# A long chain of layers in one kernel on one core: other start, other order around the recurrent mixer's last turns, other order of the last attention and of its gating, gate sums spread by transpositions

## The reference

```python
def mlstm_layer(h, ...):      # recurrent mixer
    proj = rms_norm(h, norm_g) @ w_in            # q,k | v | o | z | gates
    qk = silu(causal_depthwise_conv(qk, conv_w))
    ht = mlstm_chunkwise(q, k, v, i_pre, log_sigmoid(f_pre))
    ht = rms_norm(sigmoid(o) * ht, hnorm_g)
    return (ht * silu(z)) @ w_out
def dilated_layer(h, k, v, ...):   # last attention: 4 heads, 3 groups of dilation 1, 4, 16
    q, z = split(rms_norm(h, norm_g) @ w_in)
    q = apply_rope(rms_norm(q, qnorm_g), cos, sin)
    o = sum over groups of softmax-weighted dilated_window_attention(q[:, :, g], k, v, ...)
    return (o * silu(z)) @ w_out
def ple_add(h, p_l, ...):
    gate = sigmoid(rms_norm(h, norm_g) @ w_gate)
    return h + (p_l @ w_proj) * gate
```

## Time and profile before

| | us |
|---|---|
| median of 3 runs (1410.26 to 1410.67) | 1410.33 |
| profiled execution | 1411.51 |
| its span, first to last instruction | 1409.7 |
| TensorE busy | 1386.3 |
| VectorE busy | 832.8 |
| ACT busy | 603.5 |
| GpSimd busy | 192.2 |

### The profile page before, as it was taken

One profiled execution on the slowest core, in us unless ns is written; L12 is line 12 of the kernel. 1 busy time (PEld: TensorE's weight loads), 2 busy tenths in 40 slices (PEclk: granted clock), 3 DMA queues, 4 the chain that ended last, 5 costly groups with the idle time before them and its releaser, 6 DMA issues.

```text
span 1409.7 us, 17303 instructions
## 1 busy us (share of the span) xinstructions
PE 1386.3 (98%) x6796; PEld 1125.7 (80%) x6796; DVE 832.8 (59%) x1201; ACT 603.5 (43%) x921; POOL 192.2 (14%) x156
## 2 busy tenths in 40 slices
PE   7999999999999999999999999999999999999998
PEld 5777777878888888888888888877788888787786
DVE  5556656755342797624767355645464666777674
ACT  5254433433235564423444255434454545345461
POOL 3300010212212300000000121000001211244230
PEclk9999999999999999999999999999999999999999
DMA  6221322122353433332333323422124232221141
GB/s 234 75 78 58 90 76 75 61 75 82 104 171 92 134 91 110 106 98 89 93 102 97 118 81 125 123 78 68 61 79 160 90 117 96 75 67 54 45 144 65
DMA packets 37266, 135.39 MB, mean 96 GB/s; under 512 B 4400, under 2 KB 5056, under 8 KB 36672
## 3 DMA queue, kind: packets, MB, share of 16 engines
q1 hardware_dynamic: 37184, 134.28, 30.6%
HBM read 127.97 MB, written 6.29 MB: 95 GB/s over the span
## 4 chain that ended last, share of the span: by engine, by line
PE 93%; DVE 3%; ACT 2%; DMA 1%; POOL 1%; issue 1%; SPq 0%; DVEq 0%; ACTq 0%; POOLq 0%
PE ps L203 91%; PE ps L207 2%; ACT WH L187 1%; DMA raw<-in_wall 1%; DMA cv<-in_cvec 1%; DVE TT L162 1%; SPq L210 0%; POOL PB L150 0%; DVE WL L150 0%; ACT SS L200 0%; DVE SS L174 0%; POOL SQS L150 0%; ACT L200 0%; DVE QT L162 0%; ACT SQ L200 0%
## 5 line engine op out<-in xcount | busy, mean ns | idle before, releaser
L203 PE MATMUL ps<-HH,WH 128*128 128x512 f32 x1088 | 439.9, 404 | 9.4 <-DVE WL L150 8.6
L203 PE MATMUL ps<-HH,WL 128*128 128x512 f32 x1088 | 425.7, 391 | 0.0
L203 PE MATMUL ps<-HL,WH 128*128 128x512 f32 x1088 | 425.1, 391 | 0.0
L150 DVE TENSOR_TENSOR WL<-raw,WH 128x1024 fp32r<-128x1024 f32 x222 | 285.5, 1291 | 78.0 <-ACT WH L187 76.9
L187 ACT CAST WH<-raw 128x1024 fp32r<-128x1024 f32 x222 | 231.5, 1044 | 148.1 <-PE ps L203 128.8
L203 PEld LDWEIGHTS ps<-HH,WH 128*128 128x128 f32 x1088 | 205.2, 189 | 59.5 <-DVE WL L150 8.6
L203 PEld LDWEIGHTS ps<-HH,WL 128*128 128x128 f32 x1088 | 204.9, 188 | 44.3
L203 PEld LDWEIGHTS ps<-HL,WH 128*128 128x128 f32 x1088 | 205.3, 189 | 41.7 <-issue 1.7
L150 POOL TENSOR_TENSOR SQS<-SQS,SQ 128x512 f32<-128x512 f32 x54 | 83.2, 1541 | 701.4 <-ACT SQ L200 687.2
L203 PE MATMUL ps<-PH,WH 128*128 128x512 f32 x424 | 168.1, 396 | 0.8 <-DVE PL L150 0.8
L203 PE MATMUL ps<-PH,WL 128*128 128x512 f32 x424 | 165.2, 390 | 0.0
(11 more groups left out here) (219 smaller groups left out, 1451.5 us busy)
## 6 DMA issues: line engine op xcount, KB each, us to landing
raw<-in_wall SPq DMA_DIRECT2D x222, 512.0 KB, 3.6
kept<-PW SPq DMA_DIRECT2D x2, 2048.0 KB, 9.1
PWR<-kept SPq DMA_DIRECT2D x2, 2048.0 KB, 8.5
X<-in_xT SPq DMA_DIRECT2D x8, 256.0 KB, 5.6
X<-in_xT SPq DMA_DIRECT2D x4, 512.0 KB, 5.3
out_T<-X SPq DMA_DIRECT2D x8, 256.0 KB, 2.0
pe<-in_pT SPq DMA_DIRECT2D x2, 512.0 KB, 4.5
DM<-in_dm SPq DMA_DIRECT2D x1, 640.0 KB, 4.2
```

Of the source, the lines that this page charges most:

```text
L150: return self.put(None if self.e is None else self.e.tensor_tensor(out, x, y, op))
L203: return self.put(None if self.e is None else self.e.matmul(out, l, r, start=start, stop=stop, skip_group_check=True))
```

## The change

The first weight unit is loaded, cast and subtracted in two halves of 512 columns, X tile 1 comes behind it, units 1 and 2 follow X tiles 1 and 3. The sums of squares of the first norm are added by VectorE, not GpSimd. While the first four output tiles run, ACT and VectorE prepare fewer units ahead (`lead = 1`). TensorE runs eleven 32-bit products of 128 x 128 on the mask `rst` before its first real product; their result isn't used. The pooling side work starts one tile later.
In the recurrent mixer `gt` is turned into columns (four small transpositions more, a copy `mcol` on ACT) and spread by four transpositions for each head. The last 16 turns come after the fourth block of the residual.
In the last attention VectorE works on a query product first and ACT squares behind it and frees the bank; the rate is 4.5 instead of 3.9; the row of reciprocals of heads 0 to 2 has another bank; head h is finished after the gate tile h + 1, head 3 within the residual, and the second operation of the gate (`v_silu2_out`) is split off and made one tile later.
The last output tile is computed in two halves of 256 tokens, each with its own chain and its own store.

```diff
@@ -338,6 +339,16 @@
+    def load_half(self, i):
+        sl = slice(512 * i, 512 * i + 512)
+        d = self.dma_start(self.raw[:, 0, sl], self.wall[0, :, sl])
+        if i == 0:
+            d.then_inc("half", sig=self.S.half, by=16)
+        else:
+            d.then_inc(("unit", 0), sig=self.S.raw[0], by=16)
+            self.u = 1
...
@@ -349,6 +360,15 @@
+    def high_half(self, i):
+        sl = slice(512 * i, 512 * i + 512)
+        if i == 0:
+            self.wait_ge(self.S.half, "half")
+        else:
+            self.wait_ge(self.S.raw[0], "unit", 0)
+            self.u = 1
+        self.copy(self.WH[:, 0, sl], self.raw[:, 0, sl]).then_inc(*((["half"], [("unit", 0)])[i]), sig=self.S.whi)
...
@@ -381,7 +413,7 @@
     def prepare(self, u, last):
-        while self.u <= min(u + AHEAD, NU - 1, last):
+        while self.u <= min(u + self.lead, NU - 1, last):
...
@@ -411,7 +443,10 @@
         if ready:
-            self.wait_ge(self.S.wlo, "unit", u)
+            if self.blk <= 4:
+                self.wait_ge(self.S.wlo, "half")
+            else:
+                self.wait_ge(self.S.wlo, "unit", u)
...
@@ -458,6 +493,20 @@
+        self.later()
+    def halves(self, names, ops):
+        held = [self.block() for _ in ops]
+        n = len(ops)
+        for i, name in enumerate(names):
+            out = self.fill(self.next_bank(), name)[:, 0:256]
+            sl = slice(256 * i, 256 * i + 256)
+            for k, (h, l, sig, key) in enumerate(ops):
+                wh, wl, u = held[k]
+                self.wait_ge(sig, *key)
+                self.passes(out, wh, wl, h[:, sl], l[:, sl], k == 0, k == n - 1,
+                            [name] * (k == n - 1) + [("unit", u)] * (u is not None and i == 1))
...
@@ -729,7 +779,7 @@
     def columns():
-        yield pe_columns(p, (SB[4], ("nc", st)), [(SQS, S.pool, ("sqs", st, 7))], [free("sqs", st)])
+        yield pe_columns(p, (SB[4], ("nc", st)), [(SQS, S.dve if st == "mix" else S.pool, ("sqs", st, 7))], [free("sqs", st)])
...
@@ -918,8 +968,10 @@
         p.wait_ge(S.ident, "ident")
-        p.wait_ge(S.dve, "gM")
-        p.matmul(s, ident[0:4, h:h + 1].to_broadcast([4, P]), gt[0:4, :], True, True).then_inc(("hd", h))
+        p.wait_ge(S.act, "mcol")
+        for t in range(4):
+            p.transpose(s[:, t * P:(t + 1) * P], mcol[:, 4 * t + h:4 * t + h + 1].to_broadcast([P, P]), ident)
+        p.then_inc(("hd", h))
...
@@ -963,6 +1015,7 @@
             p.transpose(s[:, 16 + 4 * t:20 + 4 * t], gf[0:4, t * P:(t + 1) * P], ident)
+            p.transpose(s[:, 32 + 4 * t:36 + 4 * t], gt[0:4, t * P:(t + 1) * P], ident)
...
@@ -994,7 +1049,7 @@
             if n == 3:
-                r = p.fill(SB[3], ("ar", h))
+                r = p.fill(SB[4 if h < 3 else 3], ("ar", h))
...
@@ -1034,14 +1089,19 @@
         values(15)
+    s = p.fill(SB[4], ("idle",))
+    p.wait_ge(S.pool, "rst")
+    for _ in range(11):
+        p.matmul(s[:, 0:P], rst[:, 0:P], rst[:, 0:P], True, True)
+    p.then_inc("idle", free("idle"))
...
+    p.rate = 2
+    p.tile(("sk",), H_mix, SB[2])
...
-    p.rate = 2
-    p.tile(("sk",), H_mix, SB[2])
...
@@ -1128,11 +1188,16 @@
                 turn(1, i, (0, 1, 2), SB[1 + i])
-    for i in range(4):
-        turn(1, i, (3,), SB[1 + i])
...
-    p.mark("gated")
-    residual("a", O_y, 2)
+    def last_turn(k, i):
+        if (k, i) == (1, 1):
+            for i in range(4):
+                turn(1, i, (3,), SB[1 + i])
+            p.mark("gated")
+    residual("a", O_y, 2, last_turn)
...
@@ -1162,13 +1227,11 @@
         p.tile(("z", h), H_b)
-        if h < 2:
-            until(h)
+        if h:
+            until(h - 1)
...
-        if (k, i) == (0, 2):
-            until(2)
-        elif (k, i) == (1, 2):
+        if (k, i) == (1, 2):
...
@@ -1210,6 +1273,8 @@
+def v_silu2_out(v, tile):
...
@@ -1285,9 +1350,9 @@
     u, gn = qt(h, g), c("qnorm")
-    v_turned(v, name, u, ps(*name), gn, S.act, "rope sq", name)
+    v_turned(v, name, u, ps(*name), gn, S.pe, *name)
...
-    v.scalar_tensor_tensor(u, ps(*name), gn, CS[:, 0, :], MUL, MUL).then_inc(("rope u", name), free(name))
+    v.scalar_tensor_tensor(u, ps(*name), gn, CS[:, 0, :], MUL, MUL).then_inc(("rope u", name))
...
@@ -1620,6 +1685,22 @@
             v.scalar_tensor_tensor(X[:, m, :], tt_(*tg), 0.5, X[:, m, :], MUL, ADD).then_inc(("x " + (nxt or "out"), m), free("T", tg))
+        if not nxt:
+            tg = ("pg", layer, 7)
+            v.tile(8)
+            v.take("TH", tg)
+            v.take("T", tg)
+            for i in range(2):
+                sl = slice(256 * i, 256 * i + 256)
+                v.wait_ge(S.pe, *tg, i)
+                v.wait_ge(S.act, "rs", st)
+                v.tensor_tensor(th_(*tg)[:, sl], ps(*tg, i)[:, 0:256], RS[:, sl], MUL).then_inc(("th in", tg, i), free(tg + (i,)))
+                v.wait_ge(S.act, "tanh", tg, i)
+                v.wait_ge(S.again[layer], "again")
+                v.scalar_tensor_tensor(tt_(*tg)[:, sl], th_(*tg)[:, sl], 1.0, PWR[:, 7, sl], ADD, MUL).then_inc(("pt", layer, 7, i))
+                v.wait_ge(S.dve, "pt", layer, 7, i)
+                v.wait_ge(S.dve, "x " + st, 7)
+                v.scalar_tensor_tensor(X[:, 7, sl], tt_(*tg)[:, sl], 0.5, X[:, 7, sl], MUL, ADD).then_inc(("x out", 7, i))
...
@@ -1689,24 +1770,38 @@
     v.memset(ones, 1.0).then_inc("ones")
+    def v_sum(k):
+        v.wait_ge(S.act, "sqs in", "mix", k)
+        if k > 1:
+            v.wait_ge(S.dve, "sqs", "mix", k - 1)
+        v.tensor_tensor(SQS, SQS, sq_("mix", k), ADD).then_inc(("sqs", "mix", k), free("Q", ("mix", k)))
...
-        if k in (1, 3, 5, 6):
+        if k == 1:
+            v.low_half(0)
+            v.low_half(1)
+        if k > 1:
+            v_sum(k - 1)
+        if k in (3, 5, 6):
...
+    v_sum(7)
+    v.lead = 1
...
+    v.lead = AHEAD
...
+    v.rate = 2
+    v.tile(8)
...
-    v.rate = 2
-    v.tile(8)
...
@@ -1905,37 +2000,43 @@
     q_proj(0)
-    v.rate = 3.9
+    v.rate = 4.5
...
-    def gated(h):
+    def gate_in(h):
...
+    def gate_low(h):
+        t = ("z", h)
...
+        if h:
+            v_silu2_out(v, ("z", h - 1))
+            gate_in(h - 1)
...
-        if h < 2:
-            gated(h)
+        if h:
+            gate_low(h - 1)
...
-        if (k, i) == (0, 2):
-            gated(2)
-        elif (k, i) == (1, 2):
-            gated(3)
+        if (k, i) == (0, 1):
+            v_silu2_out(v, ("z", 3))
+        if (k, i) == (1, 2):
+            gate_in(3)
+            gate_low(3)
...
-            for _ in range(1):
-                v.step()
+            v.step()
...
@@ -2021,7 +2122,7 @@
     a.take("Q", ("rope", name))
-    a.wait_ge(S.pe, *name)
+    a.wait_ge(S.dve, "rope u", name)
...
@@ -2195,6 +2296,7 @@
         a.copy(acol, ps("acols")[:, 0:16]).then_inc("acol")
+        a.copy(mcol, ps("acols")[:, 32:48]).then_inc("mcol")
...
@@ -2239,6 +2341,13 @@
             a.tile(8)
+            if m == 7 and not nxt:
+                tg = ("pg", layer, 7)
+                for i in range(2):
+                    sl = slice(256 * i, 256 * i + 256)
+                    a.wait_ge(S.dve, "th in", tg, i)
+                    a.activation(th_(*tg)[:, sl], th_(*tg)[:, sl], ACT.Tanh, scale=0.5).then_inc(("tanh", tg, i))
+                continue
...
@@ -2295,16 +2404,19 @@
         a_high(a, "mix", k, "mix_pre", HH, S.x[k], "x")
-        if k in (0, 1, 3, 5):
+        if k == 0:
+            a.high_half(0)
+            a.high_half(1)
+        if k in (1, 3, 5):
...
+    a.lead = 1
...
+    a.lead = AHEAD
...
-    pool = pool_side()
-    a.side.append(pool)
...
@@ -2646,17 +2757,17 @@
     g.wait_ge(S.cvec, "cvec")
-    g_sum(g, "mix")
...
+    g.rate = 2
+    g.tile(8)
...
-    g.rate = 2
-    for _ in range(6):
+    for _ in range(5):
...
@@ -2759,13 +2867,15 @@
     load_x(0)
+    s.load_half(0)
+    s.load_half(1)
+    load_x(1)
...
-    for k in (1, 2, 3):
+    for k in (2, 3):
...
-    s.load()
...
@@ -2849,10 +2959,14 @@
     ple()
-    for m in range(8):
+    for m in range(7):
...
-    s.wait_n(S.out, 16 * 8)
+    for i in range(2):
+        sl = slice(256 * i, 256 * i + 256)
+        s.wait_ge(S.dve, "x out", 7, i)
+        s.dma_start(a_in["out"][:, 7, sl], X[:, 7, sl]).then_inc(("out", 7, i), sig=S.out, by=16)
+    s.wait_n(S.out, 16 * 9)
...
```

More of the change, by code:

```diff
@@ L2548, in between @@
                 elif k < 2:
-                    for _ in range(1):
-                        a.step()
+                    a.step()
             residual("z", 4, 3, "p1", "ple1", 1, "attended", "kv", between)
```

54 lines of the change are left out of this document (33 added, 21 removed).

## The result

The changed kernel takes 1399.13 us, median of four runs (1398.38 to 1399.54), beside 1410.36 us for the kernel before on the same chip (1410.26 to 1410.67). The ratio is 0.9919 (0.9907 to 0.9931). The forecast was 1399.0 us. The profiled execution took 1399.36 us with a span of 1397.6 us, 12.1 us shorter than the one of before. That total hides four terms that were off, up and down, so it is taken apart by place. One execution of a variant (ACT's square first in all twelve query tiles) ran at a granted clock of 0.65 and took 1986 us; it is left out of that variant's numbers.

A forecast was written before the change was run, and what follows sets the result against it. TensorE, busy 98% of the span, was taken as the bound. Gains of 4.65 (start), 1.7 (gate sums), 1.35 (turns), 2.5 (attention) and 1.15 us (tail) made 11.35 us off the 1410.33 us median: 1399.0 us, range 1395.3 to 1403.2.

The forecast's parts named there:

- First product earlier: Kernel start: loading and casting the first unit in halves moves TensorE's first product from 8.61 to 7.1 us, gain 1.5 us.
- Pace of the first products: First eight blocks: small products raise the clock; block 8 moves to 13.0 us, 2.4 us gained together with the earlier start.
- Norm: First norm: shorter lead frees ACT of a late cast, TensorE's idle time falls from 1.32 to 0.66 us, gain 0.65.
- Clock behind the norm: Right after the first norm: with half the idle time the clock doesn't fall to 0.50, gain 1.6 us, bounds 0 and 1.6.
- Gate sums: Recurrent mixer's gate heads: transpositions replace four products of 4x512, gain 1.7 us on TensorE's path, bounds 1.5 and 2.4.
- Last turns: Recurrent mixer's end: four residual blocks run before the last turns and cover the wait for HU, gain 1.35 us.
- Attention: Last attention: VectorE-first query order and 4.5 steps per tile cut idle time from 5.5 to 3.0 us, gain 2.5 us.
- Tail: Last output tile in halves: shorter final chain and store, against 0.1 us more for 48 half products, gain 1.15 us.
- bare loads: Rival, chance 0.07: in the tail each 256-column product shows its weight load, 10.4 instead of 5.5 us; total 1403.9 us.
- The clock not held: Rival, chance 0.12: at the start small products don't raise the clock, or shorter idle still lowers it; 1401.7 us.
- ACT held: Rival, chance 0.18: in the attention, squares behind VectorE cost as much as the order gives; attention gain 0, 1401.5 us.
- The loss at the first query tile: Attention's first query tile: TensorE's transpositions of the squares come only after QT and ACT's square, loss 1.05 us.

The follow-up runs named there:

- the combined run: Changed kernel with low parts of units 1 to 3 ahead of the sums and, in the first query tile only, ACT's square first: 1395.41 us.
- the first of these edits alone: Changed kernel with VectorE subtracting the low parts of units 1 to 3 one step earlier, ahead of the sums of squares: 1397.51 us.

## Why the prediction came out right

The forecast of the median was right to 0.1 us, and that is luck: errors of up to 1.85 us in its terms cancelled. The medians lie 11.2 us apart, the two profiled executions 12.1 us (that of before was 1.2 us above its median, that of after 0.2), and the sum was 11.35 us. Against the profiled ones its terms were not right: the start was 1.85 us too high, the gate sums 1.3 and the attention 1.4 us too low, and the tail 0.2 us too high. By its steps:

- **First product earlier:** 1.6 for 1.5 us. The halves land and are cast as worked out; the first real product came at 7.01 us for 7.1. The closeness is chance: in the other traces it came at 6.43 to 7.48 us.
- **Pace of the first products:** the step that failed. "If the clock is high by 7.1 us" held. But "I add these up from ACT's pace [...] and get 13.0 us" summed durations and left out idle time: VectorE stood 1.65 us for HH 1, which was late with X tile 1, and 1.41 us for ACT's square; ACT stood 1.25 us for that X tile. Block 8 came at 14.54 us. Both steps gave 1.06 us instead of 2.4 (1.0 to 1.6 us over the seven traces with this order), and the small products at most 0.4 of it. With the low part put first, the combined run reached block 8 at 12.47 us, with X tile 1 on time by chance; the first of these edits alone reached it at 13.11 us.
- **Norm:** the size was right (0.66 us of idle time instead of 1.32), the reason wrong. I named "the shorter lead"; the run with the whole lead has the same 0.66 us. The sums on GpSimd were the cause: beside them VectorE's subtraction takes 2.30 us, without them 1.22, and ACT stands up to 3.05 us for them; either can be why ACT is in a late cast. The shorter lead itself lost 0.3 us near 44.8 us, which the forecast didn't have. The Trainium skill (SBUF — State Buffer, Who interferes with whom) says that VectorE and GpSimd share a pair of ports which one of them holds for a whole instruction, against a VectorE operation with two inputs in SBUF too. The trace agrees that the two slow each other: the subtraction has two inputs in SBUF, HL takes 1.77 us instead of 0.75, and GpSimd's additions 1.6 to 2.1 us instead of 1.3. I had costed the sums at 0.7 us each on VectorE with no credit for what they give back.
- **Clock behind the norm:** 1.6 us gained, as counted, in the profiled execution. That half the idle time keeps the clock is not shown: 1.60 us idle was followed by no fall.
- **Gate sums:** a term mis-sized, 3.0 for 1.7 us. I took busy times, 4.5 and 12.1 us. The busy time of a group holds the fill of its last product, which lies under the next one: four transpositions are 0.60 us busy and put 0.35 us on the path. The product of 4x512 holds TensorE 1.05 us, nearly all that it is busy. A difference of start times was to be had from the trace of before; I didn't look.
- **Last turns:** 1.5 for 1.35 us, no wait in its place.
- **Attention:** 3.9 for 2.5 us in all. The loss at the first tile came to the place and size (1.1 us). "Left over: about 1.2 us" was wrong: the end of the stage has no wait. The new wait of 0.5 us for SQS behind the stage wasn't foreseen. And the parts were weighed wrongly: I had the order of the squares pay for the 0.9 us on PB; by the runs the rate does this too, and the order is a net loss of 0.7 us. Idle time in the stage (4.5 us gone) isn't the whole of it either: each stop adds a restart (at block 8 an idle time of 1.44 us put 1.6 us more than usual between two starts), and from the first query tile to the last residual the lead grew by 5.6 us.
- **Tail:** 0.95 for 1.15 us. The spacing is 0.12 us, not 0.11 (0.3 instead of 0.1 us lost), and the chain and store gave 1.4 instead of 1.25 us.

Of the rivals, the bare loads are out: the half products start 0.12 us apart, where the rival had 0.217. That is against the rule on loads weighed ahead of the result (the Trainium skill, TensorE: Matmul & The Clock Gate, Packing small matmuls), though the same section also lets a load go ahead of running products when it goes to the background weight buffer. The clock not held is out: the full pace was there before the first real product, and the clock didn't fall behind the norm. ACT held came half true: the order of the squares cost more than it gave, as that rival says, but at one tile only (at 1202 us ACT stands 3.1 us, and TensorE waits for its square nowhere else), and the rate made the attention gain all the same. The loss at the first query tile was where I had put it; those of 0.3 us near 44.8 us and 0.65 us at the last gate I hadn't foreseen.

## What to carry to other kernels

Price work on a full engine by the distance between the starts of its neighbours, never by its busy time: that is the difference between 1.7 and 3.0 us here. When a start is paced by transfers, write the idle times of each engine into the chain, and put what the bound engine waits for first ahead of what is only due later: one reordering of VectorE gave 1.1 us at block 8, and only together with the clock warm-up; neither moved block 8 alone, so two fixes for one place must be tried together before one is dropped. And when several edits sit at one place, don't credit the one that was meant for it: the lead did nothing for the norm and lost 0.3 us elsewhere, and the order of the squares lost 0.7 us.

## What the runs showed of the hardware

- Eleven 32-bit products of 128 columns on the mask, from 1.5 to 6.1 us, were followed after 0.9 us of idle time by products 0.24 us apart; without them the first ten are 0.43 us apart. The trace's clock records begin where the pace rises, at 5.47 us with the small products (their passes go from 0.21 to 0.11 us apart) and at 11.73 us without; before that there is no record, and the view's 1.00 says nothing.
- VectorE's subtraction of 1024 columns from two tiles in SBUF takes 1.22 us alone and 2.30 us beside GpSimd's additions of 512 columns, which take 1.3 us alone and 1.6 to 2.1 us beside VectorE.
- A product of 256 columns with its own load starts 0.12 us after the one before, one of 512 columns 0.227 us.
- A 32-bit product of 4x512 holds TensorE for 1.05 us, 4.6 times the 0.227 us of a large one; four transpositions of a broadcast column hold it 0.35 us.
- The clock fell behind an idle time of 1.32 us in the trace of before, and neither behind 0.66 us in eleven traces nor behind 1.60 us in one. What decides is open.
